# Row sums carried in extra columns of the summed rows, and the last stage shared out anew between ScalarE and VectorE

## The chip, the cores and the metric

One Trainium2 chip, of which the kernel uses one core. The metric is the time of one execution in device microseconds (µs), the median of several runs. The engines are TensorE (PE in the profile, its weight loads PEld), VectorE (DVE), ScalarE (ACT), GpSimd (POOL) and SyncE (SP, which only issues transfers). Sixteen DMA engines move data between HBM and SBUF.

## The reference

One decoder layer over 2048 prompt rows and 8 sample rows of 1024 numbers, in float32. What matters here is its second half: h is a layer norm, each row of h is sent to two of 32 small experts, and the output is a layer norm of alpha * h plus the experts' answers.

```python
h = layer_norm(ALPHA * x + mix, ln1_g, ln1_b)
f = hier_moe(h)            # top-1 group, top-2 experts in it, gates
y = layer_norm(ALPHA * h + f, ln2_g, ln2_b)

def layer_norm(x, g, b):
    mu = mean(x); var = mean((x - mu) ** 2)
    return (x - mu) * rsqrt(var + LN_EPS) * g + b

def run_block(xb, e):      # 128 rows of one expert
    return (silu(xb @ w1[e]) * (xb @ w3[e])) @ w2[e]
```

## The kernel before

The 2056 rows are 17 tiles: 16 of 128 rows, and one of 8 rows (the samples). Each engine has a program of its own, written out in order by hand; the engines meet at semaphores only. The stages in order of time are: input projection with convolution, attention, **routing** (output projection, first layer norm, router), **experts**, and the **last stage** (second layer norm).

**Routing.** A step of this loop takes one tile. VectorE's `norm_h` and `finish_h` make h in a buffer `r`; SyncE's `store_h` writes it to HBM twice, once as `h_rows`, from which the experts' rows are gathered, and once as `sum_rows` (`acc_dram`), in which the sums grow. TensorE's `router` multiplies the turned rows of h by the router's weights `wr` (36 columns: 4 groups and 32 experts) into the PSUM bank `M0`, and VectorE's `route_top` copies them out and picks. At the stage's end TensorE runs dummy matmuls (`keep_awake`) while the tables of the experts' blocks are made.

**Experts.** A block is 128 rows; here there are 39 blocks. TensorE multiplies (`up`, `turn_g`, `down`). ScalarE copies the weights of the block's second half to a fixed place (`copy_up`, L1256, and `copy_down`, L1262). The result of a block lies in `bank_S`. Its left half is scaled by the row's gate and copied to the buffer `ye` by ScalarE (`result`, L1238), its right half by VectorE (`result`, L1735). GpSimd then adds `ye` to the rows of `sum_rows` by an indirect DMA that accumulates (`add_rows`, L1930). GpSimd issues the gathers of the rows too.

**Last stage.** When the last adds have landed, SyncE loads the 17 tiles of `sum_rows` (L642) into `out_t`, in six groups with a semaphore each (`LANDED`: tiles 0, 1, 2 and 3, 4 to 6, 7 to 11, 12 to 16). A tile then needs: its statistics; the centring `(z - mean) * gain` on VectorE (`centred`, L1779); 1/sqrt(variance) by a power on GpSimd for several tiles at once (`roots`, L1956, groups `RSTD`); and the closing, times 1/sqrt and plus bias. The work is divided by lists of tile numbers:

```python
STATS_V = (0, 2, 4, 6, 9, 13)                      # statistics by VectorE: L1768, L1770, L1772
LAST_V = (2, 3, 5, 6, 8, 10, 11, 12, 13, 14)       # closing by VectorE: finished, L1786
LAG = 4                                            # a closing is issued 4 tiles behind its centring
```

The statistics of the other 11 tiles are ScalarE's: a copy of the 1024 columns that also sums them (L1297), a scaling of the sum to the mean (L1299), a square of the 1024 columns about the mean that sums (L1301), and variance plus epsilon (L1303). The closing of the other 7 tiles goes by two engines: ScalarE multiplies (`scaled`, L1311) and GpSimd adds the bias over 1024 columns (L1965). SyncE stores the tiles in the order of their numbers (L650), each when its closing is done.

Of the kernel before, what the change touches and what calls it, by code (L numbers as in the profile page):

```python
# [109 lines left out]
def laid_out(inputs):  # L110
# [55 lines left out]
ln2_in c_in0 c_in1 c_in2 c_in3 c_in4 c_in5 c_vv c_va c_rs c_dg c_z c_yp c_yv c_out  # L166
# [3 lines left out]
def layer(nc, a, o, scratch):  # L170
    with ExitStack() as ctx:
# [24 lines left out]
        out_t = view(big[:, 0:(NT + 1) * D], t=NT + 1, n=D)  # L196
# [7 lines left out]
        wr = sb("wr", KD * (NG + NE))  # L204
        wr_v = view(wr[:, :], k=KD, n=NG + NE)
# [102 lines left out]
        FOUR = ([b[:, 512 * i:512 * (i + 1)] for b in (bank_S, bank_T) for i in range(2)], [b[:, :] for b in (P0, P1, M0, M1)])  # L308
        PAIRS_IN = NT // 2 - 1
# [11 lines left out]
        ye = take(RING * D)  # L321
# [16 lines left out]
        c_st = view(take(12 * (NT + 1)), t=NT + 1, n=12)  # L338
# [3 lines left out]
        c_sum = take(2 * (NT + 1))  # L342
# [9 lines left out]

        def rank_of(t, chosen):
            return sum(u <= t for u in range(NT + 1) if chosen(u))

        def stats_by_v(t):
            return t in STATS_V

        def last_by_v(t):
            return t in LAST_V  # L360

# [17 lines left out]
        def rows_of(tile):  # L379
            return DEC if tile == NT else P  # L380
# [26 lines left out]
        def _(sp):  # L407
# [120 lines left out]
            def store_h(c):  # L528
# [75 lines left out]
            store_h(NT)  # L604

# [52 lines left out]
        def _(pe):  # L658
# [213 lines left out]
            def router(c):  # L872
# [4 lines left out]
                for k in range(KD):  # L877
                    last = mm(M0[0:n, 0:NG + NE], hT[:, k, 0:n], wr_v[:, k, :], start=(k == 0), stop=(k == KD - 1))  # L878
# [190 lines left out]
        def _(act):  # L1069
# [163 lines left out]
            def result(b, j, j6):  # L1233
# [4 lines left out]
                fn(ye[:, j * D:j * D + 512], bank_S[:, 0:512], ACT.Copy, scale=own[:, j6, 1:2]).then_inc(s["y_ev0"], 1)  # L1238
# [54 lines left out]
            def stats(t):  # L1293
# [7 lines left out]
                fn(c_sq[0:n, :], zz, ACT.Square, bias=c_mv[0:n, t, 0:1], scale=-1.0, accum_out=c_sum[0:n, 2 * t + 1:2 * t + 2])  # L1301
                act.drain()
                fn(c_ve[0:n, t:t + 1], c_sum[0:n, 2 * t + 1:2 * t + 2], ACT.Identity, bias=C["eps"][0:n, :], scale=1.0 / D  # L1303
# [701 lines left out]
```

## Time and profile before

| | µs |
|---|---|
| median of 3 runs (lowest, highest) | 1414.37 (1411.07, 1414.95) |
| the profiled execution: its time | 1409.33 |
| the profiled execution: its span | 1407.4 |
| TensorE busy in the span | 1293.1 (92%) |
| VectorE busy | 694.0 (49%) |
| ScalarE busy | 560.4 (40%) |
| GpSimd busy | 491.4 (35%) |

The span is what the trace covers; the time is measured around it. The busy shares are means over stages with different limits, so the views of the next section but one are each of one stage.

### The profile page before, as it was taken

Reading aid. Unit: us, or ns where it says so; the run is one execution under the profiler, and the core shown is the slowest. Engines: PE = TensorE matmul, PEld = TensorE weight load, DVE = VectorE, ACT = ScalarE, POOL = GpSimd, SP = SyncE. Lnnn points to the kernel's source line nnn. Section 1 sums busy time; section 2 is a strip of 40 time slices with the busy share of each in tenths; the row PEclk is TensorE's granted clock in tenths of the full one; section 3 lists DMA queues with packets and bytes.
Section 4 is the critical chain, followed back from the end, with each engine's and each line's share of the span. In section 5 each row is a group of like instructions: output and inputs, shape, how many; then the busy total and the mean of one; then the engine's idle time right before and its main releaser. Section 6 shows DMA issues by size and latency. Waiting matters only on the chain.

```text
span 1407.4 us, 21232 instructions
## 1 busy us (share of the span) xinstructions
PE 1293.1 (92%) x5597; PEld 624.0 (44%) x5598; DVE 694.0 (49%) x2021; ACT 560.4 (40%) x844; POOL 491.4 (35%) x647
## 2 busy tenths in 40 slices
PE   8999998989999988899999999999999999999700
PEld 3444445656666655355555555333333333333200
DVE  2424343444556545576666655344444444444268
ACT  0001001434445434333333331366656666566364
POOL 5113110000000000455555543455666566655233
PEclk9999999999999999999999999999999999999955
DMA  6364533121211183345554322269899999999474
GB/s 256 109 225 142 169 121 121 67 78 65 76 68 61 46 262 105 119 183 185 181 179 164 126 83 90 96 193 341 258 333 372 325 294 304 359 370 329 95 308 179
DMA packets 79393, 261.69 MB, mean 186 GB/s; under 512 B 11328, under 2 KB 30336, under 8 KB 66150
## 3 DMA queue, kind: packets, MB, share of 16 engines
q1 hardware_dynamic: 62295, 216.28, 42.4%
q0 software_dynamic: 14192, 40.94, 12.3%
q10 hardware_dynamic: 2823, 3.53, 0.8%
q8 instruction: 32, 0.52, 0.2%
q14 instruction: 51, 0.42, 0.1%
HBM read 202.17 MB, written 62.78 MB: 188 GB/s over the span
## 4 chain that ended last, share of the span: by engine, by line
PE 60%; issue 28%; DMA 4%; DVE 3%; ACT 1%; POOL 1%; DVEq 1%; POOLq 1%; SPq 1%; ACTq 1%
PE P L1018 13%; PE bank_S L1040 9%; PE M L1018 6%; PE P L860 6%; PE bank_S L860 5%; PE bank_S L687 4%; PE P L687 3%; PE P L890 2%; PE bank_T L687 2%; PE M L687 2%; DMA work<-conv_rows 2%; PE M L878 2%; PE M L1026 1%; DMA big<-sum_rows 1%; PE bank_T L869 1%
## 5 line engine op out<-in xcount | busy, mean ns | idle before, releaser
L1256 ACT ACTIVATE big<-big 128x2048 f32 x78 | 148.9, 1910 | 150.4 <-issue 103.9
L1018 PE MATMUL P<-big,work 128*64 x416 | 188.0, 595 | 0.0
L1019 PE MATMUL P<-big,work 128*64 128x512 f32 x416 | 188.0, 596 | 0.0
L1919 POOL DMA_INDIRECT work<-h_rows,piece_idx x156 | 149.6, 959 | 78.0 <-issue 55.1
L726 PE MATMUL P<-big,work 128*128 128x256 f32 (+1 forms) x512 | 174.3, 498 | 0.0
L1040 PE MATMUL bank_S<-big,work 128*64 x312 | 142.0, 598 | 3.1 <-ACT big L1262 3.1
L1042 PE MATMUL bank_S<-big,work 128*64 128x512 f32 x312 | 142.0, 599 | 0.0
L1858 POOL TENSOR_SCALAR work<-work 128x1 f32<-128x1 f32 (+1 forms) x17 | 3.8, 221 | 373.8 <-DVE work L1463 373.8
L726 PEld LDWEIGHTS P<-big,work 128*128 128x128 f32 x512 | 97.7, 195 | 70.9 <-issue 64.2
L860 PE MATMUL P<-big,work 128*128 128x512 f32 x256 | 114.9, 603 | 3.5 <-DVE work L1494 3.5
L860 PE MATMUL bank_S<-big,work 128*128 128x512 f32 x256 | 113.3, 596 | 0.0
L1018 PEld LDWEIGHTS P<-big,work 128*64 128x64 f32 x416 | 54.9, 137 | 107.7 <-issue 104.7
L1018 PE MATMUL M<-big,work 128*64 x208 | 94.2, 595 | 0.0
L1019 PE MATMUL M<-big,work 128*64 128x512 f32 x208 | 94.2, 596 | 0.0
L1040 PEld LDWEIGHTS bank_S<-big,work 128*64 128x64 f32 x312 | 43.0, 138 | 92.8 <-issue 92.6
L1262 ACT ACTIVATE big<-big 128x2048 f32 x39 | 74.4, 1909 | 21.3 <-issue 20.4
L1716 DVE STREAM_TRANSPOSE work<-work 128x1024 f32<-128x1024 f32 x39 | 79.6, 2041 | 3.3 <-DMA work<-h_rows,piece_idx 3.2
L1086 ACT ACTIVATE work<-work 128x512 f32<-128x512 f32 (+1 forms) x17 | 10.7, 630 | 176.1 <-DVE work L1363 135.3
L1098 ACT ACTIVATE work<-work 128x256 f32<-128x256 f32 x128 | 63.4, 496 | 41.3 <-DVE work L1400 41.3
L860 PEld LDWEIGHTS P<-big,work 128*128 128x128 f32 x256 | 48.1, 193 | 58.3 <-issue 54.6
L1729 DVE COPY work<-M 128x256 f32<-128x256 f32 x39 | 16.6, 424 | 111.7 <-PE M L1026 111.7
L860 PEld LDWEIGHTS bank_S<-big,work 128*128 128x128 f32 x256 | 47.5, 191 | 53.6 <-issue 53.5
(305 smaller groups left out, 2294.7 us busy)
## 6 DMA issues: line engine op xcount, KB each, us to landing
big<-in_w SPq DMA_DIRECT2D x96, 1024.0 KB, 10.5
work<-in_xt_prompt SPq DMA_DIRECT2D x32, 512.0 KB, 3.7
big<-in_toe SPq DMA_DIRECT2D x16, 512.0 KB, 3.4
work<-in_x_prompt SPq DMA_DIRECT2D x16, 512.0 KB, 4.0
h_rows<-work SPq DMA_DIRECT2D x16, 512.0 KB, 2.7
sum_rows<-work SPq DMA_DIRECT2D x16, 512.0 KB, 3.7
big<-sum_rows SPq DMA_DIRECT2D x16, 512.0 KB, 8.5
out_y_prompt<-big SPq DMA_DIRECT2D x16, 512.0 KB
```

What stands on the lines that cost most here:

```text
L687: last = mm(dst, lhs[:, k, :], rhs[:, k, :], start=(first and k == 0), stop=(final and k == KD // 2 - 1), skip_group_check=not first)
L726: last = mm(dst[0:n, 0:c1 - c0], lhs[:, k, :], w_qkv[:, k, c0:c1], start=(k == 0), stop=(k == KD - 1))
L860: last = mm(OUT[c][half][0:n, :], lhs[:, k, :], w_out[:, k, half * 512:(half + 1) * 512], start=(k == 0), stop=(k == KD - 1))
L1018: mm(lower, xgT[j][:, k, 0:U], both[:, k], start=(k == 0), stop=(k == KD - 1))
L1019: last = mm(upper, xgT[j][:, k, U:P], w_up[:, k], start=(k == 0), stop=(k == KD - 1))
L1040: mm(bank_S[0:U, cols], gT[:, k, 0:U], wmem[:, bass.ds(off + 2 * KD * FF + k * D + half * 512, 512)], start=(k == 0), stop=(k == 1))
L1042: last = mm(bank_S[U:P, cols], gT[:, k, U:P], w_dn[:, k, cols], start=(k == 0), stop=(k == 1))
L1098: fn(smx[:, i, :], smx[:, i, :], ACT.Exp, bias=nm[:, c0 + i:c0 + i + 1], scale=SCALE, accum_out=rs[:, c0 + i:c0 + i + 1])
L1256: fn(w_up.rearrange("p k m f -> p m k f")[:, :, ks, :], src, ACT.Copy).then_inc(s[f"wu{part}_ok"], 1)
L1262: fn(big[:, 2 * KD * FF:WCOLS], wmem[:, bass.ds(off + 2 * KD * FF, 2 * D)], ACT.Copy).then_inc(s["wd_ok"], 1)
L1716: nc.vector.transpose(xgT[j].rearrange("p k (i t) -> p i k t", i=4), xg[j].rearrange("p (i f k) -> p i k f", i=4, k=KD)).then_inc(s["xgT_e ...
L1919: g.indirect_dma_start(xg[j][:, 256 * i:256 * (i + 1)], None, h_pieces, bass.IndirectOffsetOnAxis(ap=piece_idx[:, j, i // 2, i % 2:i % 2 + ...
```

## The change

`sum_rows` becomes 16 columns wider: `AW = D + 16`, 1040 numbers or 4160 bytes a row. Column 1024 carries the sum of the left 512 columns' share, column 1025 that of the right 512; the rest is zero. They are made on the way:

- The router's weights get a 37th column of ones, so the router's matmuls also give the row sum of h. `route_top` copies it to a small buffer `hsum` (128 x 16), and SyncE stores it beside the row (`store_sum`, 17 more stores of 64 bytes a row), three tiles behind.
- The two result copies of an expert block also sum what they copy (`accum_out`) into two extra columns of `ye`, and the accumulating DMA carries these with the row.
- In the last stage the loads are 1040 columns wide. ScalarE makes the statistics of all 17 tiles: a copy of the two sum columns, scaled by 1/1024, that sums them to the mean; then square and epsilon as before. VectorE does all 17 centrings and all 17 closings, closings 3 tiles behind (`LAG = 3`). GpSimd makes only the powers, now for two tiles at a time.

```diff
+AW = D + 16
+NR = NG + NE + 1
...
-        out_t = view(big[:, 0:(NT + 1) * D], t=NT + 1, n=D)
+        out_t = view(big[:, 0:(NT + 1) * AW], t=NT + 1, n=AW)
...
+        hsum = [prod7[:, (AW - D) * i:(AW - D) * (i + 1)] for i in range(2)]
...
-        RSTD = ((0, 2), (2, 5), (5, 9), (9, 13), (13, NT), (NT, NT + 1))
-        STATS_V = (0, 2, 4, 6, 9, 13)
-        LAST_V = (2, 3, 5, 6, 8, 10, 11, 12, 13, 14)
-        LAG = 4
+        RSTD = tuple((t, min(t + 2, NT)) for t in range(0, NT, 2)) + ((NT, NT + 1),)
+        LAG = 3
...
+            def store_sum(c):
+                tile = OUT_IN[c]
+                n = rows_of(tile)
+                after(sp, s["ro_ev"], c)
+                sp.dma_start(acc_dram[P * tile:P * tile + n, D:AW], hsum[c % 2][0:n, :]).then_inc(s[f"sum_out{c % 2}"], 16)
...
+                if c >= 3:
+                    store_sum(c - 3)
                 if c >= 1:
                     store_h(c - 1)
...
             store_h(NT)
+            for c in range(NT - 2, NT + 1):
+                store_sum(c)
...
-                    last = mm(M0[0:n, 0:NG + NE], hT[:, k, 0:n], wr_v[:, k, :], start=(k == 0), stop=(k == KD - 1))
+                    last = mm(M0[0:n, 0:NR], hT[:, k, 0:n], wr_v[:, k, :], start=(k == 0), stop=(k == KD - 1))
...
-                fn(ye[:, j * D:j * D + 512], bank_S[:, 0:512], ACT.Copy, scale=own[:, j6, 1:2]).then_inc(s["y_ev0"], 1)
+                at = j * AW
+                fn(ye[:, at:at + 512], bank_S[:, 0:512], ACT.Copy, scale=own[:, j6, 1:2], accum_out=ye[:, at + D:at + D + 1]).then_inc(s["y_ev0"], 1)
...
+            for t in range(NT + 1):
                 n = rows_of(t)
-                zz = out_t[0:n, t]
+                mean, sq = c_mv[0:n, t, 0:1], c_sum[0:n, t:t + 1]
                 landed(act, t)
-                fn(zz, zz, ACT.Copy, accum_out=c_sum[0:n, 2 * t:2 * t + 1])
+                fn(c_two[0:n, :], out_t[0:n, t, D:D + 2], ACT.Copy, scale=1.0 / D, accum_out=mean)
                 act.drain()
-                fn(c_mv[0:n, t, 0:1], c_sum[0:n, 2 * t:2 * t + 1], ACT.Copy, scale=1.0 / D)
+                fn(c_sq[0:n, :], out_t[0:n, t, 0:D], ACT.Square, bias=mean, scale=-1.0, accum_out=sq)
                 act.drain()
...
+                if c >= 2:
+                    v.wait_ge(s[f"sum_out{c % 2}"], 16 * (c // 2))
+                cp(hsum[c % 2][0:n, 0:1], M0[0:n, NG + NE:NR])
                 cp(lg8[0:n, 0:NG], M0[0:n, 0:NG])
...
-                ts(ye[:, j * D + 512:(j + 1) * D], bank_S[:, 512:], own[:, j6, 1:2], None, ALU.mult).then_inc(s["y_ev1"], 1)
+                at = j * AW
+                ts(ye[:, at + 512:at + D], bank_S[:, 512:], own[:, j6, 1:2], 0.0, ALU.mult, ALU.add,
+                   accum_out=ye[:, at + D + 1:at + D + 2]).then_inc(s["y_ev1"], 1)
...
             for step in range(NT + 1 + LAG):
                 if step <= NT:
-                    if stats_by_v(step):
-                        stats(step)
                     centred(step)
-                if step >= LAG and last_by_v(step - LAG):
+                if step >= LAG:
                     finished(step - LAG)
...
+            hold_ge(s["sum_out0"], 16 * (NT // 2 + 1))
+            hold_ge(s["sum_out1"], 16 * (NT // 2))
...
-                                     ye[:, j * D:(j + 1) * D], None, compute_op=ALU.add).then_inc(s[f"y_out{j6 % 2}"], 16)
+                                     ye[:, j * AW:(j + 1) * AW], None, compute_op=ALU.add).then_inc(s[f"y_out{j6 % 2}"], 16)
...
-                if not last_by_v(t):
-                    n = rows_of(t)
-                    g.wait_ge(s["c_z"], t + 1 - rank_of(t, last_by_v))
-                    gtt(out_t[0:n, t], out_t[0:n, t], ln_b[0:n, :], ALU.add).then_inc(s["c_yp"], 1)
```

What stands at the end of VectorE's program, first before, then in the changed kernel (L1768 to L1772 are statistics, L1779 and L1760 the centring, L1786 and L1767 the closing; c_va is ScalarE's statistics, c_rs GpSimd's power, c_in5 a group of loads):

```order
L1768 BN_STATS work<-big 128x6 [waits c_in5]
L1768 BN_STATS work<-big 128x6
L1770 BN_AGGR work<-work 128x2
L1772 TENSOR_SCALAR work<-work 128x1
L1779 SCALAR_TENSOR_TENSOR big<-big,work,lnx 128x1024
L1779 SCALAR_TENSOR_TENSOR big<-big,work,lnx 128x1024 [waits c_va]
L1786 SCALAR_TENSOR_TENSOR big<-big,work,lnx 128x1024 [waits c_rs]
L1779 SCALAR_TENSOR_TENSOR big<-big,work,lnx 128x1024 [waits c_va]
L1786 SCALAR_TENSOR_TENSOR big<-big,work,lnx 128x1024 [waits c_rs]
L1779 SCALAR_TENSOR_TENSOR big<-big,work,lnx 8x1024 [waits c_va]
L1786 SCALAR_TENSOR_TENSOR big<-big,work,lnx 128x1024 [waits c_rs] x3
```

```order
L1760 SCALAR_TENSOR_TENSOR big<-big,work,lnx 128x1024 [waits c_va]
L1767 SCALAR_TENSOR_TENSOR big<-big,work,lnx 128x1024 [waits c_rs]
L1760 SCALAR_TENSOR_TENSOR big<-big,work,lnx 8x1024 [waits c_va]
L1767 SCALAR_TENSOR_TENSOR big<-big,work,lnx 128x1024 [waits c_rs] x3
L1767 SCALAR_TENSOR_TENSOR big<-big,work,lnx 8x1024 [waits c_rs]
```

The statistics are gone from this engine, a centring and a closing alternate throughout, and the last four instructions are closings, where before they were three.

What ScalarE does from its last result copy on, first before (it skips tile 0 and begins with tile 1), then in the changed kernel:

```order
L1238 ACTIVATE work<-bank_S,work 128x512 [waits tab_ok,y_out0,pe_dn]
L1289 UNCONDITIONAL_BRANCH
L1297 ACTIVATE big,work<-big 128x1024 [waits c_in1]
L1299 ACTIVATE work<-work 128x1
L1301 ACTIVATE work<-big,work 128x1024
L1303 ACTIVATE work<-work,const 128x1
L1297 ACTIVATE big,work<-big 128x1024 [waits c_in2]
L1299 ACTIVATE work<-work 128x1
L1301 ACTIVATE work<-big,work 128x1024
L1303 ACTIVATE work<-work,const 128x1
L1311 ACTIVATE big<-big,work 128x1024 [waits c_rs,c_dg]
```

```order
L1297 ACTIVATE work<-big 128x2 [waits c_in0]
L1299 ACTIVATE work<-big,work 128x1024
L1301 ACTIVATE work<-work,const 128x1
L1297 ACTIVATE work<-big 128x2 [waits c_in1]
L1299 ACTIVATE work<-big,work 128x1024
L1301 ACTIVATE work<-work,const 128x1
L1297 ACTIVATE work<-big 128x2 [waits c_in2]
```

A tile takes three instructions with one pass over 1024 columns, where it took four with two passes; tile 0 comes first, and no multiplication for a closing stands between the tiles.

## Rows read from the trace of the kernel before

**Rows 1.** Busy time per engine in two stretches: expert stage, last stage.

```profile
1100.00:1200.00 100.00, 100.00 (x464) 33.67 (x460) 43.33 (x91) 61.70 (x46) 61.31 (x109) 1.00 0.95 305
1347.00:1402.50 55.50, 0.00 (x0) 0.00 (x0) 53.09 (x51) 35.95 (x68) 25.52 (x13) 0.50 0.59 238
```

**Rows 2.** Waits between 860 and 1345: total, times, longest.

```profile
ACT big L1256 <- DMA big<-in_w: 31.6, 16, 3.6
PE bank_S L1040 <- ACT big L1262: 3.1, 1, 3.1
```

**Rows 3.** The page's group of ScalarE's copies L1262.

```profile
L1262 ACT ACTIVATE big<-big 128x2048 f32 x39 | 74.4, 1909 | 21.3 <-issue 20.4
```

**Rows 4.** Two pieces of the chain that ended last: start, us, what.

```profile
1345.44 12.34 DMA big<-sum_rows
...
1401.17 1.29 DVE big L1786
```

**Rows 5.** Groups of the last stage, shapes kept apart: busy, mean ns.

```profile
L1779 DVE SCALAR_TENSOR_TENSOR big<-big,work,lnx 128x1024 f32<-128x1024 f32 x16 | 24.6, 1561 | 0.0
L1786 DVE SCALAR_TENSOR_TENSOR big<-big,work,lnx 128x1024 f32<-128x1024 f32 x10 | 16.7, 1668 | 0.9
```

**Rows 6.** Timeline of the last stage, VectorE and GpSimd.

```profile
1347.12 1.29 DVE L1768 BATCH_NORM_STATS2 work<-big 128x6 f32<-128x512 f32 x2 [14.85 <-issue]
1348.83 2.47 DVE L1779 SCALAR_TENSOR_TENSOR big<-big,work,lnx 128x1024 f32<-128x1024 f32 x2
1349.19 1.51 POOL L1956 TENSOR_TENSOR work<-work,const 128x2 f32<-128x2 f32 x1 [14.53 <-DVE work L1772]
...
1390.45 1.28 DVE L1779 SCALAR_TENSOR_TENSOR big<-big,work,lnx 128x1024 f32<-128x1024 f32 x1
1391.82 1.29 DVE L1786 SCALAR_TENSOR_TENSOR big<-big,work,lnx 128x1024 f32<-128x1024 f32 x1
1392.99 2.34 POOL L1965 TENSOR_TENSOR big<-big,lnx 128x1024 f32<-128x1024 f32 x1 [3.43 <-ACT big L1311]
1393.02 3.38 DVE L1779 SCALAR_TENSOR_TENSOR big<-big,work,lnx 8x1024 f32<-8x1024 f32 x1
```

**Rows 7.** Timeline of the last stage, ScalarE.

```profile
1347.60 1.06 ACT L1297 ACTIVATE big<-big 128x1024 f32<-128x1024 f32 x1 [0.37 <-DMA big<-sum_rows]
...
1366.30 1.15 ACT L1301 ACTIVATE work<-big,work 128x1024 f32<-128x1024 f32 x1
...
1367.81 1.04 ACT L1297 ACTIVATE big<-big 128x1024 f32<-128x1024 f32 x1
...
1369.01 0.20 ACT L1299 ACTIVATE work<-work 128x1 f32<-128x1 f32 x1
1369.29 1.15 ACT L1301 ACTIVATE work<-big,work 128x1024 f32<-128x1024 f32 x1
```

**Rows 8.** Timeline of the last expert blocks.

```profile
1322.52 0.69 ACT L1238 ACTIVATE work<-bank_S,work 128x512 f32<-128x512 f32 x1 [3.05 <-PE bank_S L1042]
1323.81 1.91 ACT L1262 ACTIVATE big<-big 128x2048 f32 x1 [0.61 <-issue]
...
1331.41 0.69 ACT L1238 ACTIVATE work<-bank_S,work 128x512 f32<-128x512 f32 x1 [5.68 <-PE bank_S L1042]
1331.52 0.75 DVE L1735 TENSOR_SCALAR work<-bank_S,work 128x512 f32<-128x512 f32 x1 [7.81 <-PE bank_S L1042]
...
1333.11 1.55 POOL L1930 DMA_INDIRECT sum_rows<-work,idx  x1 [0.43 <-issue]
...
1339.44 10.14 SPq L642 DMA_DIRECT2D big<-sum_rows  x17
```

**Rows 9.** Timeline of the routing stage's end, queue of SyncE.

```profile
862.77 0.43 SPq L533 DMA_DIRECT2D sum_rows<-work  x1
```

**Rows 10.** Timeline of the routing stage's end, VectorE.

```profile
860.36 0.08 DVE L1571 DVE_READ_ACCUMULATOR2_ANT work<- 128x1 f32 x1
...
869.61 0.16 DVE L1518 COPY work<-M 128x4 f32<-128x4 f32 x1 [0.62 <-PE M L878]
```

More of the change, by code:

```diff
@@ L320, in layer @@
         gT = view(take(FF), k=2, t=P)
-        ye = take(RING * D)
+        ye = take(RING * AW)
         lists = take(2 * U * UN)
@@ L341, in layer @@
         c_rs = take(NT + 1)
-        c_sum = take(2 * (NT + 1))
+        c_sum = take(NT + 1)
+        c_two = take(2)
         c_sq = xgT[0].rearrange("p k t -> p (k t)")
         LANDED = ((0, 1), (1, 2), (2, 4), (4, 7), (7, 12), (12, NT + 1))
-        RSTD = ((0, 2), (2, 5), (5, 9), (9, 13), (13, NT), (NT, NT + 1))
-        STATS_V = (0, 2, 4, 6, 9, 13)
-        LAST_V = (2, 3, 5, 6, 8, 10, 11, 12, 13, 14)
-        LAG = 4
+        RSTD = tuple((t, min(t + 2, NT)) for t in range(0, NT, 2)) + ((NT, NT + 1),)
+        LAG = 3
         def part_of(t, parts):
             return [lo <= t < hi for lo, hi in parts].index(True)
[L353 to L360, printed above, removed]
         def landed(eng, t):
@@ L1290, in _ @@
                 result(NB - 1, (NB - 1) % RING, (NB - 1) % UN)
[L1293 removed]
+            for t in range(NT + 1):
                 n = rows_of(t)
[L1295 removed]
+                mean, sq = c_mv[0:n, t, 0:1], c_sum[0:n, t:t + 1]
                 landed(act, t)
[L1297 removed]
+                fn(c_two[0:n, :], out_t[0:n, t, D:D + 2], ACT.Copy, scale=1.0 / D, accum_out=mean)
                 act.drain()
[L1299 removed]
+                fn(c_sq[0:n, :], out_t[0:n, t, 0:D], ACT.Square, bias=mean, scale=-1.0, accum_out=sq)
                 act.drain()
[L1301 to L1317 removed]
+                fn(c_ve[0:n, t:t + 1], sq, ACT.Identity, bias=C["eps"][0:n, :], scale=1.0 / D).then_inc(s["c_va"], 1)
         @block.vector
@@ L1631, in _ @@
             v.wait_ge(s["ln1_in"], 48)
+            for b in range(2):
+                v.memset(hsum[b], 0.0)
             for c in range(NT + 4):
@@ L1697, in _ @@
             n_blocks = v.value_load(nblk_i[0:1, :], min_val=FEWEST, max_val=NB)
+            for j in range(RING):
+                v.memset(ye[:, j * AW + D + 2:(j + 1) * AW], 0.0)
             def listed(b, j, j6, n, added=None):
@@ L1760, in _ @@
                         result(b - 1, (j - 1) % RING, (j - 1) % UN, 3 * i + (j - 1 - RING) // 2)
-            def stats(t):
-                n = rows_of(t)
-                zz = out_t[0:n, t]
-                landed(v, t)
-                for i in range(2):
-                    nc.vector.bn_stats(c_st[0:n, t, 6 * i:6 * i + 6], zz[:, 512 * i:512 * (i + 1)])
-                v.drain()
-                nc.vector.bn_aggr(c_mv[0:n, t], c_st[0:n, t])
-                v.drain()
-                ts(c_ve[0:n, t:t + 1], c_mv[0:n, t, 1:2], EPS / ALPHA ** 2, None, ALU.add).then_inc(s["c_vv"], 1)
             def centred(t):
                 n = rows_of(t)
-                if not stats_by_v(t):
-                    v.wait_ge(s["c_va"], t + 1 - rank_of(t, stats_by_v))
-                zz = out_t[0:n, t]
-                stt(zz, zz, c_mv[0:n, t, 0:1], ln_g[0:n, :], ALU.subtract, ALU.mult).then_inc(s["c_dg"], 1)
+                after(v, s["c_va"], t)
+                zz = out_t[0:n, t, 0:D]
+                stt(zz, zz, c_mv[0:n, t, 0:1], ln_g[0:n, :], ALU.subtract, ALU.mult)
             def finished(t):
@@ L1949, in _ @@
                 g.wait_ge(s[f"w{m}_ld"], 16 * NE)
[L1951 to L1952 removed]
+            for lo, hi in RSTD:
                 n = rows_of(lo)
[L1954 to L1955 removed]
+                after(g, s["c_va"], hi - 1)
                 gtt(c_rs[0:n, lo:hi], c_ve[0:n, lo:hi], C["mhalf"][0:n, :].broadcast_to([n, hi - lo]), ALU.pow).then_inc(s["c_rs"], 1)
[L1958 to L1965 removed]
 INS = {
```

50 lines of the change are left out of this document (13 added, 37 removed).

## The prediction

> **What bounds the kernel now.** I read the stages first, since shares over the whole span mix them. In the expert stage TensorE is busy for all of 100 µs, ScalarE for 61.70, VectorE for 43.33, and the DMA engines for 0.95 of the time [rows 1]. The waits of that stretch say the same: the one long wait of TensorE is 3.1 µs, once, for ScalarE's weight copy L1262 [rows 2]. What VectorE and ScalarE get on top in that stage is free as long as it stays inside their idle time; the DMA engines have little left. In the last stage it is the other way round: TensorE is done, the DMA engines are at 0.59, ScalarE at 35.95 of 55.5 µs, and VectorE at 53.09 of 55.5 [rows 1]. The chain ends with a wait for loaded tiles and, last of all, a closing of VectorE at 1401.17 + 1.29 = 1402.46 [rows 4]. So the last stage is VectorE's, from 1347.12 to 1402.46, 55.3 µs. The span ends 4.9 µs later with the last stores.
>
> Why are 27 passes and 6 tiles of statistics 53 µs? An undisturbed centring or closing takes 1.28 to 1.29 µs [rows 6]. But the 16 centrings have a mean of 1561 ns and the 10 closings one of 1668 ns [rows 5]. With the 8-row centring of 3.38 they sum to 24.6 + 16.7 + 3.4 = 44.7 µs, where 27 x 1.28 would be 34.6. The timeline shows where the other 10.1 µs are: the 3.38 µs centring starts 0.03 µs after GpSimd's bias addition L1965 of 2.34 µs [rows 6]; it takes the sum of the two, less little. VectorE stood still while GpSimd worked on 1024 columns.
>
> **The last stage, worked out.** The change takes from VectorE the statistics and, by taking GpSimd's seven additions away, the 10.1 µs of standing still; it adds 7 closings, 9.0 µs. The end has to be laid out in order, since VectorE now depends on ScalarE for every tile.
>
> ScalarE's pace: from a square to the next tile's first instruction is 1367.81 - 1366.30 = 1.51 µs, which holds square, its sum's read, epsilon [rows 7]. The new first instruction, a 128 x 2 copy that sums, does not exist before. Lower bound: the 128 x 1 scaling, 1369.29 - 1369.01 = 0.28 start to start, and nothing for the sum. Upper bound: the 1024-column copy that sums, 1369.01 - 1367.81 = 1.20. It is nearest to the first; that copy's sum costs about 0.08 beyond its end (1367.81 + 1.04 = 1368.85, next start 1369.01, against 0.08 behind the scaling), so I take 0.28 + 0.1 = 0.4. A tile is then 1.9 µs, and its statistics are out about 2.0 after its start.
>
> VectorE's pace: centring to closing is 1391.82 - 1390.45 = 1.37 (a drain lies between), closing to next centring 1393.02 - 1391.82 = 1.20, so 2.57 a tile [rows 6]. That is slower than ScalarE's 1.9; beyond the first tiles VectorE sets the end.
>
> The start: tiles 2 and 3 landed at 1347.6, where ScalarE had waited 0.37 for them [rows 7]. I put 0.4 on this (below), so ScalarE begins tile 2 at 1348.0 and tile 3 at 1349.9, and tile 3's statistics are out at 1351.9. Had ScalarE begun tile 0 as late as its loops may let it, this would be 1352.3. I take 1352.2 for the centring of tile 3. VectorE itself is there at 1347.12, after 14.85 of issue with no wait in it, the branches of unused blocks [rows 6], and does centrings 0 to 2 in between. From tile 3 on: 13 x 2.57 = 33.4 gives the last centring at 1385.6; closing 13 follows 1.37 behind and closings 14 to 16 at the same step, since each has the drain, the last at 1391.1, done at 1392.4. Tiles 7 to 11 had landed when the chain's wait ended at 1345.44 + 12.34 = 1357.8 [rows 4], and ScalarE gets to tile 7 at about 1357.5, so the loads cost at most 0.3 on an engine that then runs ahead. **Before 1402.5, now 1392.4: -10.1 µs.** A cross-check by amounts: 34 passes at a mean step of 1.285 are 43.7, and the wait for the first three tiles 1.5, from 1347.3 to 1392.5.
>
> Behind the last closing: before, tiles 14, 15 and 16 all waited for closing 14 and went out together, in 4.9 µs. Now tile 15 leaves 1.4 µs ahead of the last, which is 8 rows, 32 KB. I estimate 4.0, **-0.9 µs**; bounds 0 and -1.6.
>
> A rule of the Trainium skill speaks against GpSimd's powers, which become nine instead of six (SBUF — State Buffer, section SBUF: two separate sides): GpSimd and a VectorE instruction with two SBUF inputs exclude each other, and the loser waits for the whole instruction. The additions above agree. For the powers the trace does not: a power of 1.51 µs lay over the start of the second of two centrings, and both together took 2.47, the undisturbed time [rows 6]. By the rule the sum would be up to 9 x 1.51 = 13.6 µs worse; by the row, nothing. I go by the row, and keep the rule as a rival.
>
> **The drain of the experts.** The last blocks are a chain: result copy 1322.52, weight copy 1323.81 behind it in ScalarE's order, TensorE, result copies 1331.41 and 1331.52, adding DMA issued 1333.11, loads from 1339.44 [rows 8]. Each sum adds its read: 0.1 on the copy before the weight copy, 0.1 on the last ones (VectorE's read of an accumulator is 0.08 [rows 10]; the multiply reads PSUM as before, and I take its 0.75 as unchanged). The adding DMA carries 1.6% more, under 0.1. Together +0.3; bounds 0 and +1. With 0.1 for wider loads these are the 0.4 above.
>
> **In the expert stage itself**: 39 blocks [rows 3] get 0.1 µs more on ScalarE, 38% idle, and on VectorE, more so; nothing. The DMA engines get 64 bytes more on each 4096 added, at most 1.6% of one of three kinds of traffic. ScalarE waited for weights 16 times, 31.6 µs in all [rows 2], and TensorE never noticed; 0.
>
> **Routing.** One more column for 8 matmuls, one more copy of one column (0.08 to 0.16, as L1518) on VectorE, one more wait, one more store in SyncE's queue a tile. Behind `store_sum` stand h's stores and the loads of the tile after next; what it waits for (ro_ev) was signalled one of VectorE's steps before the h that the next store needs, so it holds nobody. VectorE's wait for a free `hsum` is tightest for the last tile: the store of tile number 14 goes behind h's last store, 862.77 + 0.43 = 863.2 [rows 9], and is needed at 869.61 [rows 10], 6.4 µs for 8 KB. If it came later, the last tile's routing and the dummy matmuls behind it would wait. Other waits of TensorE for VectorE here are each under a µs. **+0.2**; bounds 0 and +1. GpSimd's two new waits lie ahead of the first gather, which needs block lists that SyncE loads behind those same stores; 0.
>
> **Sum**: -10.1 (with the +0.3 and +0.1 in it) - 0.9 + 0.2 = -10.8 µs. The profiled execution would go from 1409.33 to 1398.5. It was 5 µs under the median of the three runs, so I take the difference, not the level: 1414.37 - 10.8 = **1403.6 µs**.
>
> **Rivals.**
> *ScalarE sets the pace* (8%). If the 128 x 2 copy costs 1.20, a tile is 2.71, over VectorE's 2.57. Begun at 1344.5, tile 16's statistics are out at 1344.5 + 16 x 2.71 + 2.8 = 1390.7, closing 16 ends at 1390.7 + 4 x 1.37 + 1.29 = 1397.5: -5.0 instead of -10.1, **1408.7**. Against it: two columns.
> *The powers block VectorE* (3%), the rule above: 1403.6 + 13.6 = **1417**. It speaks for it that the additions did; against it the 2.47.
> *Wider rows make the adding DMAs dear* (7%, the slower side). ScalarE's 46 instructions in 100 µs at five a block are 9.2 blocks, 10.9 µs each, of which the DMA engines are idle for 5%, 0.54 µs [rows 1]. Extra time of an add above 0.54 holds the weights back, then TensorE, 39 times; the gain is gone at 0.54 + 10.8/39 = 0.82 µs. An add takes 1339.44 - (1333.11 + 1.55) = 4.8 µs from the end of its issue to the first load [rows 8]. If a row became two packets and that cost a fifth, 0.96, the result is 1403.6 + 39 x 0.42 = **1420**. Against it: bytes grow by 1.6%, which is 0.08. The Trainium skill bears on this (DMA: Bandwidth & Descriptors, SWDGE vs HWDGE vs iDMA): GpSimd's DMAs prefer packets of at most 4096 bytes. By it a row of 4160 would be cut, and this rival's chance is what I give that; no run shows it, since all rows here were 4096.
> *The same with an extra of 0.7 to 0.9* (6%): about **1413**, no change.
> The forecast has 76%.
>
> Two runs of this kernel differ by up to 0.3% (1411.07 to 1414.95), and under that, 4.2 µs, I call it the same. Faster: forecast and ScalarE's pace, 0.84. Same: 0.07. Slower: 0.09. The range goes from 1399.5 (a gain of 12 and a favourable median) to 1410 (ScalarE's pace, and 1.3); it leaves out the DMA and power cases, 16%.
>
> **What would show it.** In the last stage: VectorE steps of 1.37 and 1.20 throughout and none over 2 µs; ScalarE 1.9 a tile and done near 1378; the last closing near 1392.4 and the end 4.0 behind. Under the result copies: 0.69 and 0.75 unchanged, each with a short read of its sum behind it. In the experts: blocks of 10.9 µs and TensorE with no waits. I am wrong if the 128 x 2 copy is over 1 µs, if centrings of 2 to 3 µs stand beside powers, if loads start later than 1340.5, or if blocks get longer.

## The result, and the profile after

The changed kernel takes 1401.76 µs (median of 4 runs, 1395.9 to 1402.99), the kernel before 1414.66 µs (4 runs, 1411.07 to 1416.96). The ratio is 0.9907, 95% interval 0.988 to 0.9934: 13 µs faster, where 10.8 was forecast. The profiled execution took 1402.51 µs with a span of 1400.6, against 1409.33 and 1407.4.

Below, the last stage is measured from one point that every kernel has: R, the start of ScalarE's last result copy. It is at 1331.41 before [rows 8] and at 1337.27 after. First, busy time by stretch of the changed kernel: stretch, its length, then TensorE, its weight loads, VectorE, ScalarE and GpSimd, then granted clock, DMA share and GB/s.

```profile
1100.00:1200.00 100.00, 100.00 (x462) 33.78 (x460) 43.84 (x101) 61.43 (x57) 61.30 (x110) 1.00 0.95 305
1352.00:1398.20 46.20, 0.00 (x0) 0.00 (x0) 42.47 (x34) 27.24 (x78) 9.56 (x9) 0.50 0.79 322
```

The expert stage is as it was [rows 1]. VectorE has 42.47 µs of work in the last stage where it had 53.09, in 34 instructions, and GpSimd 9.56 for 25.52. Next, the groups of the last stage with shapes kept apart (busy µs, mean ns, idle time before them and what ended it), which answer to [rows 5]:

```profile
L1767 DVE SCALAR_TENSOR_TENSOR big<-big,work,lnx 128x1024 f32<-128x1024 f32 x16 | 20.5, 1284 | 1.2
L1760 DVE SCALAR_TENSOR_TENSOR big<-big,work,lnx 128x1024 f32<-128x1024 f32 x16 | 20.4, 1283 | 16.3 <-ACT work L1301 16.3
L1299 ACT ACTIVATE work<-big,work 128x1024 f32<-128x1024 f32 x16 | 18.4, 1148 | 1.1
L1935 POOL TENSOR_TENSOR work<-work,const 128x2 f32<-128x2 f32 x8 | 8.7, 1087 | 33.8 <-ACT work L1301 33.8
L1297 ACT ACTIVATE work<-big 128x2 f32<-128x2 f32 x16 | 3.1, 192 | 13.2 <-DMA big<-sum_rows 13.2
```

Centrings (L1760) and closings (L1767) have means of 1283 and 1284 ns, where they had 1561 and 1668: none stands still any more. The timeline of ScalarE and VectorE (start, µs, what, and in brackets the idle time before) shows the pipeline that answers to [rows 6, 7, 8]:

```profile
1337.27 0.69 ACT L1238 ACTIVATE work<-bank_S,work 128x512 f32<-128x512 f32 x1 [5.64 <-PE bank_S L1041]
1337.39 0.75 DVE L1727 TENSOR_SCALAR_CACHE_REDUCE work<-bank_S,work 128x512 f32<-128x512 f32 x1 [7.76 <-PE bank_S L1041]
1337.85 0.19 ACT L1238 ACTIVATION_READ_ACCUMULATOR work<-bank_S,work 128x1 f32 x1
1338.07 0.08 DVE L1727 DVE_READ_ACCUMULATOR work<-bank_S,work 128x1 f32 x1
1339.01 1.55 POOL L1911 DMA_INDIRECT sum_rows<-work,idx  x1 [0.40 <-issue]
1345.95 11.01 SPq L644 DMA_DIRECT2D big<-sum_rows  x17
1353.27 2.51 DVE L1760 SCALAR_TENSOR_TENSOR big<-big,work,lnx 128x1024 f32<-128x1024 f32 x2 [15.12 <-ACT work L1301]
1354.34 0.20 ACT L1297 ACTIVATE work<-big 128x2 f32<-128x2 f32 x1 [1.20 <-DMA big<-sum_rows]
1354.45 0.19 ACT L1297 ACTIVATION_READ_ACCUMULATOR work<-big 128x1 f32 x1
1354.70 1.15 ACT L1299 ACTIVATE work<-big,work 128x1024 f32<-128x1024 f32 x1
1356.21 0.19 ACT L1297 ACTIVATE work<-big 128x2 f32<-128x2 f32 x1
1358.20 1.32 DVE L1760 SCALAR_TENSOR_TENSOR big<-big,work,lnx 128x1024 f32<-128x1024 f32 x1 [0.57 <-ACT work L1301]
...
1388.90 1.28 DVE L1760 SCALAR_TENSOR_TENSOR big<-big,work,lnx 128x1024 f32<-128x1024 f32 x1
1390.25 1.28 DVE L1767 SCALAR_TENSOR_TENSOR big<-big,work,lnx 128x1024 f32<-128x1024 f32 x1
1391.45 1.27 DVE L1760 SCALAR_TENSOR_TENSOR big<-big,work,lnx 8x1024 f32<-8x1024 f32 x1
1392.79 5.40 DVE L1767 SCALAR_TENSOR_TENSOR big<-big,work,lnx 128x1024 f32<-128x1024 f32 x4
1398.22 0.30 SPq L649 DMA_DIRECT2D out_y_sample<-big  x1
```

Read it so. The 128 x 2 copy and its read take 0.36 µs until the square (1354.34 to 1354.70), and a tile takes 1.87 (1354.34 to 1356.21). VectorE alternates with steps of 1.35 and 1.20. It waited for ScalarE before tile 3 (0.57, at 1358.20), and from there on it sets the pace. The row of four closings, all but the last with 128 rows, ends at 1392.79 + 5.40 = 1398.19, and the span 2.4 µs later.

Of 76.0 µs from R to the span's end (1407.4 - 1331.41) 63.3 are left (1400.6 - 1337.27): **-12.7**. The span fell only by 6.8, since R came 5.9 later in this execution. The first 8-row router matmul, which marks the start of routing, was 2.5 later (608.00 against 605.52), so 2.5 of the 5.9 arose ahead of routing, where the change does no more than load a router matrix one column wider and longer rows of zeros. The other 3.4 arose between there and R (729.3 against 725.9); below it is seen whether that is the change's.

### The profile page after: what moved, and what is told of

Read it like the earlier page. It is cut to its first block, busy times and chain, and to the rows that moved or that the text cites. A ratio compares the mean times of both kernels' runs of the same rounds, so it can differ in the third digit from the quotient of the medians.

```text
span 1400.6 us, 21325 instructions
## 1 busy us (share of the span) xinstructions
PE 1297.0 (93%) x5597; PEld 624.9 (45%) x5598; DVE 684.6 (49%) x2065; ACT 553.8 (40%) x895; POOL 477.0 (34%) x643
## 3 DMA queue, kind: packets, MB, share of 16 engines
q0 software_dynamic: 14192, 41.26, 12.3%
## 4 chain that ended last, share of the span: by engine, by line
PE 57%; issue 28%; DMA 6%; DVE 4%; ACT 1%; DVEq 1%; SPq 1%; POOL 1%; POOLq 1%; ACTq 0%
PE P L1017 12%; PE bank_S L1039 10%; PE M L1017 6%; PE P L859 5%; PE bank_S L859 4%; PE bank_S L686 4%; DMA work<-conv_rows 3%; PE P L686 3%; PE P L889 3%; PE bank_T L686 2%; PE M L686 2%; PE M L877 1%; PE M L1025 1%; DMA big<-sum_rows 1%; ACT work L1299 1%
## 5 line engine op out<-in xcount | busy, mean ns | idle before, releaser
L1262 ACT ACTIVATE big<-big 128x2048 f32 x39 | 74.4, 1908 | 13.0 <-issue 11.8
```

Source lines behind the costliest of these rows:

```text
L1262: fn(big[:, 2 * KD * FF:WCOLS], wmem[:, bass.ds(off + 2 * KD * FF, 2 * D)], ACT.Copy).then_inc(s["wd_ok"], 1)
```

## The experiments

Each run was profiled once, and some were timed over several executions. One table for all. The columns are distances in the trace in µs: R to the end of the last closing, from there to the span's end (behind), the two together (sum), from the start of the issue of the last adding DMA to the first load, and from the start of routing to R. The last column is the median time in µs, with its ratio to the kernel before, run beside it.

| kernel | R to last closing | behind | sum | add to load | routing to R | time, ratio to before (95%) |
|---|---|---|---|---|---|---|
| before | 71.0 | 5.0 | 76.0 | 6.33 | 725.9 | |
| changed | 60.9 | 2.4 | 63.3 | 6.94 | 729.3 | 1401.76; 0.9907 (0.988 to 0.9934) |
| changed, again | 60.6 | 2.4 | 63.0 | 6.97 | 726.8 | 1397.37; 0.9912 (0.9881 to 0.9943) |
| e1 split only | 69.3 | 2.4 | 71.7 | 6.09 | 725.9 | 1406.18; 0.9971 (0.9947 to 0.9995) |
| e2 carry only | 71.6 | 4.9 | 76.5 | 6.64 | 725.9 | 1406.6; 0.9991 (0.9963 to 1.0018) |
| e3 additions back | 73.5 | 2.4 | 75.9 | 6.39 | 723.6 | 1408.77, one run |
| e4 17 powers | 60.5 | 2.4 | 62.9 | 6.60 | 727.0 | 1398.9, one run |
| e5 few drains | 58.5 | 2.6 | 61.1 | 6.59 | 725.8 | 1392.68, one run |
| e5 again | 59.4 | 2.6 | 62.0 | 7.07 | 729.2 | 1397.34; 0.9916 (0.9886 to 0.9946) |
| e6 small tile first | 59.7 | 3.3 | 62.9 | 6.82 | 724.6 | 1392.58, one run |
| e7 other load groups | 61.2 | 2.4 | 63.7 | 6.76 | 725.5 | 1397.88, one run |
| e8 e5 and e7 | 59.4 | 2.6 | 62.0 | 6.77 | 725.3 | 1397.44; 0.9899 (0.9883 to 0.9915) |
| e9 e5 and e6 | 58.4 | 3.3 | 61.7 | 6.48 | 730.4 | 1397.64; 0.9908 (0.9876 to 0.9939) |
| e12 e9, early drains back | 58.6 | 3.3 | 61.9 | 6.75 | 726.7 | 1404.17, one run |

Medians of the kernel before beside them differ by chip: 1410.76 for e1 to e4, 1412.44 for e5 to e8, 1408.33 for e9 and the two repeats; the one run beside e12 took 1411.53.

Two profiles of the same kernel differ by 3.4 µs between routing and R (e5: 725.8 and 729.2), and by 7.7 ahead of it (routing begins at 603.87 and 611.58). This goes along with TensorE's granted clock. Busy time by stretch of these two profiles, first e5, then its repeat (columns as above, the clock third from the end):

```profile
500.00:600.00 100.00, 85.42 (x400) 47.51 (x399) 55.21 (x199) 37.22 (x101) 17.95 (x20) 1.00 0.53 166
500.00:600.00 100.00, 85.02 (x381) 47.52 (x382) 49.42 (x187) 36.58 (x99) 14.28 (x14) 0.91 0.52 164
```

With TensorE equally busy, the first had the full 2.4 GHz throughout, the second a mean of 0.91, some of the stretch at 1.2 GHz, and it got through fewer matmuls. Over the fourteen profiles the time at 1.2 GHz ahead of routing, by the traces' record of the granted clock, lies between 10 and 34 µs, and the start of routing moves with it (600.8 and 603.2 where it is 14 and 10, 610.9 and 613.7 where it is 34). A single time therefore tells nothing of 1 or 2 µs in the last stage, and the distances from R do, to some 0.5 to 1 µs.

**e1: the division of work without the sums.** The kernel before, with every statistic ScalarE's (in its old four instructions, two passes), and every closing VectorE's. GpSimd's loop is reduced to the powers. The lists, against the kernel before:

```diff
-        RSTD = ((0, 2), (2, 5), (5, 9), (9, 13), (13, NT), (NT, NT + 1))
-        STATS_V = (0, 2, 4, 6, 9, 13)
-        LAST_V = (2, 3, 5, 6, 8, 10, 11, 12, 13, 14)
-        LAG = 4
+        RSTD = tuple((t, min(t + 2, NT)) for t in range(0, NT, 2)) + ((NT, NT + 1),)
+        STATS_V = ()
+        LAST_V = tuple(range(NT + 1))
+        LAG = 3
...
```

> The kernel before (1024 columns, no sums carried) with the last stage shared out as in the change: ScalarE makes the statistics of all 17 tiles, still by a copy of 1024 columns that sums (1.20 us), scaling (0.28) and square (1.51), VectorE all centrings and closings, GpSimd only powers. My theory is that the carried sums are what keeps ScalarE ahead of VectorE: without them a tile is 2.99 us, over VectorE's 2.57, so ScalarE sets the pace and the last closing ends some 70 us after the last result copy begins (71.1 before, 60.9 in the changed kernel), with 2.4 us behind it: about -3 us against before. Rival: taking GpSimd's additions away is what counts and the carried sums little; then 62 to 63 us and -10 us or more.

The last stage gained 4.3: 1.7 up to the last closing, and 2.6 behind it. Timeline:

```profile
1357.32 1.04 ACT L1297 ACTIVATE big<-big 128x1024 f32<-128x1024 f32 x1
1357.45 1.31 DVE L1779 SCALAR_TENSOR_TENSOR big<-big,work,lnx 128x1024 f32<-128x1024 f32 x1 [1.70 <-ACT work L1303]
...
1360.30 1.04 ACT L1297 ACTIVATE big<-big 128x1024 f32<-128x1024 f32 x1
1360.43 1.28 DVE L1779 SCALAR_TENSOR_TENSOR big<-big,work,lnx 128x1024 f32<-128x1024 f32 x1 [0.29 <-ACT work L1303]
```

A centring starts 0.13 behind ScalarE's next tile each time: ScalarE, at 1360.30 - 1357.32 = 2.98 a tile, sets VectorE's pace, which could be 2.57. VectorE waited for it 15 times. So the columns are needed because with them ScalarE's time for a tile falls below VectorE's 2.57.

**e2: the sums without the division.** All of the transport (37th column, `store_sum`, sums of the result copies, rows of 1040), and the last stage of the kernel before, which reads none of it. The lists, against the changed kernel (the code of the old last stage comes back with them):

```diff
...
-        LAG = 3
+        STATS_V = (0, 2, 4, 6, 9, 13)
+        LAST_V = (2, 3, 5, 6, 8, 10, 11, 12, 13, 14)
+        LAG = 4
...
```

> The carried sums alone: router column, sum stores, summing result copies and 1040-column rows as in the change, but the last stage of before, which reads 1024 columns of each row and makes its own sums. My theory: the transport costs next to nothing, +0.5 to +1 us against before (reads of the sums in the drain, a slightly longer last add), blocks of 10.9 us unchanged. Rival: the 5.9 us by which the changed kernel's profile was later at its last result copy come from the transport; then +4 to +6 us, and it shows between the first router matmul and the last result copy.

The last stage lost 0.5, and the whole time shows no difference. With e1 this gives 4.3 - 0.5 = 3.8 for the two parts apart, and 12.7 together: the 8.9 between are what neither has without the other. One profile of each stands behind this, so the 0.5 is within what such distances differ by.

**e3: GpSimd's additions put back.** The changed kernel, and behind each of seven powers an addition over 128 x 1024 into memory that nobody reads. Nothing waits for it, so only its presence can cost.

```diff
+                if lo < 14:
+                    g.drain()
+                    gtt(big[:, 20000:21024], big[:, 20000:21024], ln_b, ALU.add)
```

> The changed kernel, and GpSimd adds 128x1024 to 128x1024 in unused memory behind each of its first seven powers. Nobody waits for them. My theory: VectorE stands still while GpSimd adds, so centrings or closings of 3 us and more appear beside them and the last closing ends 9 to 13 us later than the 60.9 after the last result copy. Rival: before, the long instructions had another cause (the loads and stores running then); then 60.9 as in the changed kernel and all at 1.28.

Groups, then two pieces of the timeline:

```profile
L1767 DVE SCALAR_TENSOR_TENSOR big<-big,work,lnx 128x1024 f32<-128x1024 f32 x16 | 34.0, 2127 | 1.2
L1760 DVE SCALAR_TENSOR_TENSOR big<-big,work,lnx 128x1024 f32<-128x1024 f32 x16 | 20.3, 1277 | 15.5 <-ACT work L1301 15.5
L1938 POOL TENSOR_TENSOR big<-big,lnx 128x1024 f32<-128x1024 f32 x7 | 18.9, 2703 | 5.6 <-issue 5.6
```

```profile
1356.38 2.67 POOL L1938 TENSOR_TENSOR big<-big,lnx 128x1024 f32<-128x1024 f32 x1 [0.17 <-issue]
1356.92 3.21 DVE L1767 SCALAR_TENSOR_TENSOR big<-big,work,lnx 128x1024 f32<-128x1024 f32 x1
```

Seven closings became 3.2 µs long. The one shown was due at 1356.92, the addition ended at 1359.05, and it ended 1.08 behind that: it stood still until GpSimd was done and then ran. Up to the last closing this cost 73.5 - 60.9 = 12.6 µs, 1.8 for each addition. That is more than the 10.1 gained there, with everything else of the change in place.

**e4: a power for each tile**, 17 instead of 9.

```diff
-        RSTD = tuple((t, min(t + 2, NT)) for t in range(0, NT, 2)) + ((NT, NT + 1),)
+        RSTD = tuple((t, t + 1) for t in range(NT + 1))
```

> The changed kernel with a power for each tile, 17 instead of 9. By the profile's rows a power costs VectorE nothing: last closing 60.9 us after the last result copy, all passes at 1.28. Rival, by the rule that GpSimd and a VectorE instruction with two SBUF inputs exclude each other for the whole instruction: each power of about 0.9 us that meets VectorE stops it, 8 more of them +3 to +7 us.

No cost: 60.5 against 60.9, with centrings and closings of 1282 and 1284 ns:

```profile
L1935 POOL TENSOR_TENSOR work<-work,const 128x1 f32<-128x1 f32 x16 | 14.3, 895 | 27.6 <-ACT work L1301 27.6
```

Were VectorE to wait through each power, the 8 more would cost up to 7.2 µs (8 x 0.895). By the rule of the Trainium skill (SBUF — State Buffer, section SBUF: two separate sides) whichever of the two starts first keeps the other out for its whole instruction. With the additions of e3 the trace agrees. Here it does not for VectorE: passes that began beside a running power kept their 1.28. For GpSimd it does. In the changed kernel too, a power of 128 x 2 that began in the middle of a pass always ended 0.55 µs behind that pass's end (five of five):

```profile
1369.81 1.28 DVE L1767 SCALAR_TENSOR_TENSOR big<-big,work,lnx 128x1024 f32<-128x1024 f32 x1
1370.39 1.25 POOL L1935 TENSOR_TENSOR work<-work,const 128x2 f32<-128x2 f32 x1 [2.67 <-ACT work L1301]
1371.01 1.28 DVE L1760 SCALAR_TENSOR_TENSOR big<-big,work,lnx 128x1024 f32<-128x1024 f32 x1
```

The pass from 1369.81 ended at 1371.09 and the power at 1371.64, while the next pass, begun at 1371.01, lost nothing.

**e5: a drain before every third closing only**, to size what the step of 1.35 has over 1.20.

```diff
-                v.drain()
+                if t % 3 == 0:
+                    v.drain()
```

> The changed kernel with VectorE's drain ahead of every third closing only. My theory: VectorE's step sets the end of the last stage, and of its 2.57 us a tile 0.17 is the drain; 11 of 17 drains less are -1.9 us: last closing 59.0 us after the last result copy. Rival: ScalarE or the stores bind as well, then the gain is under 0.5.

Up to the last closing it gained 2.4 in the first profile (58.5 for 60.9), 0.35 of which is that loads began sooner behind the add (6.59 against 6.94). The second profile has 59.4, with loads at 7.07, so the forecast of another 58.5 (the text stands at e9) was missed. In that profile's timeline the closing without a drain follows at 1364.58 to 1365.78, 1.20, like the centring:

```profile
1363.38 1.29 DVE L1768 SCALAR_TENSOR_TENSOR big<-big,work,lnx 128x1024 f32<-128x1024 f32 x1
1364.58 1.28 DVE L1760 SCALAR_TENSOR_TENSOR big<-big,work,lnx 128x1024 f32<-128x1024 f32 x1
1365.78 1.28 DVE L1768 SCALAR_TENSOR_TENSOR big<-big,work,lnx 128x1024 f32<-128x1024 f32 x1
```

**e6: the 8-row tile first**, so that a 128-row tile is the last to be stored.

```diff
+        ORDER = [NT] + list(range(NT))
...
-            for t in range(NT + 1):
+            for p, t in enumerate(ORDER):
...
```

This holds in the loads, statistics, centrings, closings and stores alike. The powers follow: one for the small tile, then one for every two tiles.

> The changed kernel with the tile of 8 rows first in all orders of the last stage, so that the last closing and the last store are of 128 rows. It measures the term that I had too small, what lies behind the last closing (4.9 before, forecast 4.0, found 2.4). Theory: the size of the last store and how many wait for the same closing decide; 3.5 to 4 here. Rival: only the number waiting together matters; 2.4 here too.

Behind the last closing are 3.3 instead of 2.4 (3.28 and 2.42), a little under the 3.5 to 4 of the theory: the small last store is worth 0.9. Up to the last closing it is 1.3 shorter than in the first profile of the changed kernel and 0.9 shorter than in the second, so the sum is the same, 62.9.

**e7: load groups cut so that tile 2 is waited for alone**: tiles 0, 1, 2, 3 to 5, 6 to 10, 11 to 16.

```diff
-        LANDED = ((0, 1), (1, 2), (2, 4), (4, 7), (7, 12), (12, NT + 1))
+        LANDED = ((0, 1), (1, 2), (2, 3), (3, 6), (6, 11), (11, NT + 1))
```

> The changed kernel with a landing group for tile 2 alone: groups 0, 1, 2, 3 to 5, 6 to 10, 11 to 16. Before its steady run VectorE waited 0.56 and 0.57 us for the statistics of tiles 2 and 3. If these waits are what is late, last closing 60 us after the last result copy, -0.6 to -1.1; if ScalarE then waits for tile 3 instead, no change.

No gain, 61.2. ScalarE's timeline, tile 2 and then tile 3: tile 2 was taken without a wait, and the wait moved on to tile 3, whose group now ends with tile 5, and grew from 1.20 to 1.50:

```profile
1348.17 0.19 ACT L1297 ACTIVATE work<-big 128x2 f32<-128x2 f32 x1
...
1351.62 0.20 ACT L1297 ACTIVATE work<-big 128x2 f32<-128x2 f32 x1 [1.50 <-DMA big<-sum_rows]
```

**e8: few drains and these groups.**

> Both of these edits, few drains and the new landing groups, timed. If VectorE's step and start are what binds: last closing 58 to 58.5 us after the last result copy, 2.5 to 3 us less than the changed kernel, ratio to before about 0.989 where the change alone had 0.9907. Rival: nothing left to gain there, ratio 0.991.

59.4, not under e5: a miss. The groups bring nothing here either.

**e9: few drains and the small tile first; e5 and the changed kernel again, beside it.**

> The 8-row tile goes first in the last stage (a 128-row tile closes it), and a drain stands only before every third closing. If both effects add as they did apart, last result copy to last closing is 59.66 less some 2.0, 57.3 to 57.8, and 3.2 to 3.3 behind it: 60.6 to 61.1 to the end. The rival: ScalarE then sets the pace (17 tiles at 1.88 plus its start), the drains bring nothing more, and the stage stays at 62 to 63. Against the kernel before, ratio about 0.989.

> The same kernel as the one with a drain before every third closing, now timed. Last result copy to last closing 58.5 again, to the end 61.1; 2.2 us under the changed kernel in the median, ratio about 0.989 to before.

> The changed kernel again, beside the two others on one chip. Last result copy to last closing 60.9, to the end 63.3. Its median should be 2.2 us above the one with few drains, if upstream noise (5 us between single runs) averages out over the rounds; if the two medians stand within 1 us, or the other way round, the last stage's 2.2 us can't be seen in whole times.

Up to the last closing e9 has 58.4, where 57.3 to 57.8 was forecast, and behind it 3.3. Against 59.7 with all drains (e6) this is a little over half of the 2.4 that few drains brought alone. Its timeline shows 0.66 of what is missing:

```profile
1360.01 7.14 POOL L1941 TENSOR_TENSOR work<-work,const 128x2 f32<-128x2 f32 x1 [1.43 <-ACT work L1303]
```

```profile
1364.13 1.27 DVE L1772 SCALAR_TENSOR_TENSOR big<-big,work,lnx 128x1024 f32<-128x1024 f32 x1
1365.32 1.27 DVE L1763 SCALAR_TENSOR_TENSOR big<-big,work,lnx 128x1024 f32<-128x1024 f32 x1
1367.25 1.28 DVE L1772 SCALAR_TENSOR_TENSOR big<-big,work,lnx 128x1024 f32<-128x1024 f32 x1 [0.66 <-POOL work L1941]
```

A power of 128 x 2 took 7.14 µs. While it hung, VectorE ran passes at steps of 1.20 with no drain between them. The last one shown ended at 1366.59, the power at 1367.15, and the closing behind waited 0.66 for that very power. The rule of the Trainium skill named with e4 (SBUF — State Buffer, section SBUF: two separate sides) has this side too, that GpSimd is the one who waits when VectorE is first. Here the trace agrees: the power came to an end only in VectorE's pause, again 0.56 behind the end of a pass. What is new against e4 is that it missed the ends of five passes before that one.

The three medians are 1397.64, 1397.34 and 1397.37, where the forecast had few drains 2.2 ahead: the 1 to 2 µs that the last stage differs by can't be seen in whole times, and no version here is shown to beat the changed kernel. What the three agree on, beside the same runs of the kernel before, is the gain: ratios 0.9908, 0.9916, 0.9912.

**e12: e9 with the drains put back before the first five closings**, to see whether the gaps that they leave let the power in.

```diff
-                if p % 3 == 0:
+                if p <= 4 or p % 3 == 0:
```

> The kernel with the 8-row tile first and few drains, with drains put back before the first five closings (then every third). There a power of 128 x 2 took 7.14 us under six passes of VectorE with steps of 1.20 and no drain, ended in VectorE's pause, and the fourth closing waited 0.66 for it. If it is the gap that a drain leaves which lets GpSimd in, no power is over 2.5 us, no closing waits for one, and last result copy to last closing is 58.39 less 0.66 plus three drains of 0.15, about 58.2. If the long power had another cause (a chance of when it is issued), one over 3 us may stand here too, and a closing waits again; if it was ScalarE's late tile, the wait of 0.66 stays with powers of usual length.

No power is longer than 2.33 and no closing waits for one:

```profile
1362.40 2.33 POOL L1941 TENSOR_TENSOR work<-work,const 128x2 f32<-128x2 f32 x1 [1.77 <-ACT work L1303]
```

Up to the last closing it has 58.6, 0.4 over the forecast, 0.30 of it a wait of a centring for ScalarE. This power missed the end of one pass, which the next followed without a drain, and ended 0.56 behind the end of the pass at 1364.17, where a drain leaves 0.07. e6, with all its drains, has the same: its second power of 128 x 2 missed one end without a drain and ended 0.56 behind the next, at 1351.31, which has one.

```profile
1349.52 2.35 POOL L1940 TENSOR_TENSOR work<-work,const 128x2 f32<-128x2 f32 x1 [1.48 <-ACT work L1303]
```

So a gap lets in a power that is being kept out. But a gap is not always needed: the changed kernel's power above came in at an end without one (1371.09), and in e5, also with few drains, the longest power was 1.73. Powers missed whole passes only in the kernels with the 8-row tile first (e6, e9, e12), and there only early in the last stage. Why there is open.

## Why the prediction was right, step by step

- **The bound** was right: the last stage was VectorE's. From R to the end it lost 12.7 µs, and the median fell by 12.9 (1414.66 to 1401.76); in the repeat it fell by 11.0 (1408.33 to 1397.37).
- **Standing still.** That GpSimd's additions made up VectorE's 10.1 µs was read from two means and one pair of rows; e3 shows that they can, at 12.6 µs for seven. The powers cost VectorE nothing, as forecast (e4), but the row that this was read from shows less than was read from it: that power began 0.36 µs into a centring and ended 0.59 behind that centring's end, so there it was GpSimd that waited. That a running power does not hold VectorE is shown by e4's rows.
- **ScalarE's pace**: 1.9 forecast, 1.87 measured. The new copy, taken at 0.4, takes 0.36. e1 shows what the rival with ScalarE setting the pace would have been like, at 2.98 a tile.
- **VectorE's pace and the start**: steps of 1.37 and 1.20 forecast, 1.35 and 1.20 measured. Tile 3's centring came 20.9 behind R (forecast 1352.2, 20.7 behind a copy 0.1 later than before), the last centring 54.2 (forecast 54.1). -10.1 was forecast to the last closing and 71.0 - 60.9 = 10.1 was measured. That it is the same to the tenth is luck: the repeat has 71.0 - 60.6 = 10.4, and errors of either sign stand in the sum, as the next points say.
- **Behind the last closing** is the term that was mis-sized: 4.0 was forecast and 2.4 measured, -2.6 for -0.9, beyond the bound of -1.6. (The prediction has 4.9 for before; the distance is 1407.44 - 1402.45 = 4.99.) e1, which has 2.4 without any columns, shows that it comes from the division and order of the closings alone. e6 gives 0.9 of it to the size of the last store. The remaining 1.7 (5.0 to 3.3) goes with one tile left to store, and not three. Half of that is the issue of the last store, which before began 0.91 behind the last closing and now begins 0.02 behind it:

```profile
1403.36 0.73 SPq L650 DMA_DIRECT2D out_y_sample<-big  x1
```

- **The drain of the experts**: the multiply from PSUM kept its 0.75 with a read of 0.08 behind it, as forecast; ScalarE's read is 0.19, and from R to the issue of the last add it takes 1.74 for 1.70, where 0.1 more was forecast. The last add was mis-sized: with rows of 1040 from its issue to the first load it took 6.4 to 7.1, mean 6.7 over the twelve profiles that have them, against 6.33 and 6.09 in the two with 1024. That is some +0.5 where I put under 0.1; that it is the longer rows, and how, no run isolates. ScalarE began tile 2 at 17.1 behind R, where 16.5 was forecast. The centring of tile 3 came only 0.2 late, since the forecast had 0.3 of reserve there, and 13 tiles at 2.558 ((1391.45 - 1358.20)/13) instead of 2.57 gave that back.
- **The adding DMAs** did not become dear. The software queue of the changed kernel (packets, MB, share):

```profile
q0 software_dynamic: 14192, 41.26, 12.3%
```

  The software queue moved 41.26 MB for 40.94 in the same 14192 packets and the same 12.3%. A row of 4160 bytes travels as one packet. The Trainium skill (DMA: Bandwidth & Descriptors, section SWDGE vs HWDGE vs iDMA) has at most 4096 bytes to a packet "preferably"; that a longer row would be cut was my reading of it, and no cut takes place here. A block of the experts takes 10.89 µs before and after (mean of 30, from result copy to result copy). ScalarE's waits for weights have 38.5 µs for 31.6, but 32.9 in the repeat, so that is spread; TensorE waited for weights once, 0.4 µs, in both:

```profile
ACT big L1256 <- DMA big<-in_w: 38.5, 20, 3.6
```

- **Routing**: +0.2 can't be told from nothing. From its start to R the twelve profiles with the transport have a mean of 726.7 (723.6 to 730.4), the two without 725.9 both; the 3.4 of the first profile are the spread of this distance, which the same kernel showed again at 726.8. It, too, goes along with the clock: TensorE ran 10.2 µs at 1.2 GHz in this stretch in the first profile and 6.8 in that of before. Profiles with the same 6.8 have 725.9 and 725.9 without the transport and 725.8 to 727.0 with it (four, mean 726.4), so some +0.4. The tight place, the free `hsum` for the last tile, was none: its copy waited for TensorE.

```profile
874.00 0.16 DVE L1504 COPY work<-M 128x1 f32<-128x1 f32 x1 [1.44 <-PE M L877]
```

By whole times alone a cost of the transport of up to some 2 µs before R stays possible: e2's interval reaches to 1.0018, and e2's own last stage takes 0.5 of that.

## What to carry to other kernels

When two engines share a loop by tile numbers, work out each engine's pace per tile for the new division before the totals: here moving work alone gave 4.3 of the 12.7, only 1.7 of it ahead of the last closing, since ScalarE's 2.98 then ruled; only what brought it below VectorE's 2.57 released the rest. An instruction of GpSimd over 1024 columns beside two-input passes of VectorE costs VectorE its own time, so look at the mean of a group against its undisturbed instruction. And measure a change in one stage from an event inside the program: whole times could not tell 63 µs from 61.

## What the runs showed of the hardware

- An addition of GpSimd over 128 x 1024 (2.7 µs) held a closing for 1.9 µs (3.21 for 1.28), but 16 powers of 128 x 1 (mean 895 ns) held none. It is the power that gives way, and it can be kept out long: between undisturbed passes of VectorE the same 128 x 2 power took 0.69 to 1.51 µs in the changed kernel, by how far into a pass it began, and 7.14 once in e9.

```profile
1362.11 0.69 POOL L1935 TENSOR_TENSOR work<-work,const 128x2 f32<-128x2 f32 x1 [3.17 <-ACT work L1301]
...
1381.55 1.51 POOL L1935 TENSOR_TENSOR work<-work,const 128x2 f32<-128x2 f32 x1 [2.24 <-ACT work L1301]
```

- A sum taken along by a copy is cheap on both engines: a read of 0.19 µs on ScalarE that begins before the copy's end (1337.27 + 0.69 = 1337.96, read from 1337.85), and of 0.08 on VectorE.
- R moved between 1326.7 and 1340.7 over the fourteen profiles of nearly equal kernels, and most of it arose before routing (its start lay between 600.8 and 613.7), in code that is all but the same in all. It went along with the time that TensorE ran at 1.2 GHz there, 10 to 34 µs. What set that time was not looked for.
